# Sliding-window attention of block 1: two heads at a time in unrolled TensorE, VectorE and ScalarE steps, with the key projection moved first

## The reference, cut to what matters

```python
q, k, v = split(h @ w_qkv, [1024, 1280])
q = rms_norm(q per head, q_gain);  k = rms_norm(k per head, k_gain)
if latent: q, k = rope(q), rope(k)
q = q * 64 ** -0.5
s = concat(q @ kc.T, where(|t - s| <= 128, q @ kx.T, -inf))   # 512 keys
p = softmax(concat(sink, s))[1:]
o = p @ concat(vc, vx);   out = o @ w_out
```

## Time and profile before

| | us |
|---|---|
| median of 3 runs (4312.4 to 4322.81) | 4312.77 |
| the profiled execution: its own time | 4309.27 |
| the profiled execution: its span | 4307.5 |
| TensorE matmul busy | 3476.0 (81%) |
| VectorE busy | 1810.1 (42%) |
| ScalarE busy | 1109.1 (26%) |
| GpSimd busy | 1760.8 (41%) |

### The profile page before, as it was taken

How to read it: one execution, slowest core, us unless ns; L and a number is a source line. 1 busy time by engine, 2 the same in 40 slices (tenths; PEclk the granted TensorE clock), 3 DMA queues, 4 the chain that set the end, 5 groups by cost and what they waited for, 6 DMA issues and landing times.

```text
span 4307.5 us, 52062 instructions
## 1 busy us (share of the span) xinstructions
PE 3476.0 (81%) x20144; PEld 2893.3 (67%) x20144; DVE 1810.1 (42%) x2876; ACT 1109.1 (26%) x1485; POOL 1760.8 (41%) x1417
## 2 busy tenths in 40 slices
PE   6999897687875899989997566988666787776778
PEld 3777685576764577767886334988535777744677
DVE  2213386544446321232122534342256863234783
ACT  2222233111112221222222222333322332412332
POOL 1444341353442244434443003787014666403465
PEclk8999997798997999989998667998857898876889
DMA  6344221000000334333322001444202333310233
GB/s 241 137 161 140 81 97 50 1 1 1 1 1 1 107 135 163 129 121 134 115 91 102 10 0 39 161 161 143 86 9 78 117 123 131 120 59 33 104 112 112
DMA packets 58832, 388.59 MB, mean 90 GB/s; under 512 B 6432, under 2 KB 7712, under 8 KB 21184
## 3 DMA queue, kind: packets, MB, share of 16 engines
q1 hardware_dynamic: 49424, 320.49, 21.3%
q10 hardware_dynamic: 9072, 64.74, 4.2%
q0 software_dynamic: 192, 1.31, 0.1%
HBM read 385.47 MB, written 1.05 MB: 90 GB/s over the span
## 4 chain that ended last, share of the span: by engine, by line
PE 63%; DVE 13%; issue 11%; POOL 10%; ACT 1%; DMA 1%; POOLq 0%; DVEq 0%; SPq 0%; ACTq 0%
PE bank L550 15%; PE bank L551 14%; PE bank L552 14%; POOL ring_lo L1938 8%; DVE core L1844 2%; PE bank L752 2%; PE bank L750 2%; PE bank L742 1%; PE bank L575 1%; PE bank L859 1%; PE bank L845 1%; PE bank L923 1%; PE bank L568 1%; PE bank L838 1%; DVE h_hi L1441 1%
## 5 line engine op out<-in xcount | busy, mean ns | idle before, releaser
L1938 POOL TENSOR_TENSOR ring_lo<-ring,w_hi 128x512 fp32r<-128x512 f32 (+1 forms) x833 | 1086.5, 1334 | 1353.1 <-ACT w_hi L1052 1353.0
L552 PE MATMUL bank<-h_hi,ring_lo 128*128 128x256 f32 (+1 forms) x3376 | 1140.8, 338 | 0.0
L550 PE MATMUL bank<-h_hi,w_hi 128*128 128x512 f32 (+1 forms) x2448 | 885.6, 362 | 220.4 <-DVE h_lo L1443 96.2
L551 PE MATMUL bank<-h_lo,w_hi 128*128 128x512 f32 (+1 forms) x2448 | 864.6, 353 | 0.0
L552 PEld LDWEIGHTS bank<-h_hi,ring_lo 128*128 128x128 f32 x3376 | 678.8, 201 | 58.6
L550 PEld LDWEIGHTS bank<-h_hi,w_hi 128*128 128x128 f32 x2448 | 482.6, 197 | 322.0 <-issue 151.9
L551 PEld LDWEIGHTS bank<-h_lo,w_hi 128*128 128x128 f32 x2448 | 485.4, 198 | 51.1
L1052 ACT ACTIVATE w_hi<-ring 128x2048 fp32r<-128x2048 f32 (+2 forms) x227 | 394.8, 1742 | 465.2 <-PE bank L552 351.1
L552 PE MATMUL bank<-hid_r,ring_lo 128*128 128x256 f32 (+1 forms) x1088 | 365.6, 336 | 0.0
L1477 DVE SCALAR_TENSOR_TENSOR core<-core,bank 128x512 f32<-128x512 f32 (+1 forms) x88 | 54.6, 621 | 636.1 <-ACT core L1116 636.1
L550 PE MATMUL bank<-hid_r,w_hi 128*128 128x512 f32 (+1 forms) x808 | 290.5, 359 | 1.8 <-POOL ring_lo L1938 1.8
(11 more groups left out here) (347 smaller groups left out, 5916.3 us busy)
## 6 DMA issues: line engine op xcount, KB each, us to landing
ring<-w SPq DMA_DIRECT2D x88, 1024.0 KB, 4.8
zbuf<-ada_later ACTq DMA_DIRECT2D x60, 1024.0 KB, 4.8
ring<-up SPq DMA_DIRECT2D x48, 1024.0 KB, 4.8
ring<-w SPq DMA_DIRECT2D x64, 704.0 KB, 4.1
ring<-mla_in SPq DMA_DIRECT2D x30, 1024.0 KB, 4.8
ring<-down SPq DMA_DIRECT2D x32, 768.0 KB, 4.2
ring<-dn_in SPq DMA_DIRECT2D x16, 1024.0 KB, 4.8
ring<-ada SPq DMA_DIRECT2D x12, 1024.0 KB, 12.2
```

The source lines that it names most:

```text
L550: pe.matmul(out, a[0], b[0], start=start, stop=False)
L551: pe.matmul(out, a[0], b[1], start=False, stop=False)
L552: return pe.matmul(out, a[1], b[0], start=False, stop=stop)
L1938: ins = pool.tensor_tensor(like(ring_lo[:, r, a:b], part), like(ring[:, r, a:b], part), part.bitcast(F32), ALU.subtract)
```

## The change

- The columns of `swa_qk` are stored keys first, so slot 0 makes the two key chunks, and slots 1 to 4 the queries. GpSimd issues the load of the tables (`late`) ahead of its part in `swa_qk`, not behind it.
- ScalarE squares each chunk straight from PSUM as it copies it, and folds `q_gain` into the copy of a query chunk. TensorE's sums, and the rotations, stand between the slots of the projection. The sums of a query chunk are made with the squares as weights and two columns of the ones as the moving operand, which puts them on the partitions of the queries: 128 x 2 outputs for each 128 queries.
- Queries are rotated without their norm. The reciprocal root of each query and head goes into the scale of the exponential (`q_scale`), 16 columns at a time, and, negated, into its bias. Only the two key chunks still have a 512-wide reciprocal and scaling on VectorE.
- Attention is 16 pairs, written out without a loop. A pair is the two heads of one query chunk (partitions 0 to 63 and 64 to 127) and 128 queries. The mask is added on TensorE, by a matmul with the identity into the same PSUM region as the scores, for the one block of 128 keys that needs it. The maximum and the exponential read PSUM. The reciprocal of the sums is put on a diagonal (128 x 128), and a matmul of exponentials and diagonal turns and scales in one step.
- TensorE's turn t makes scores and mask of pair t, turns pair t-2, and multiplies pair t-3 with the values. Exponentials have three buffers. The chunks of `h` are split for the output projection inside the loop, and its first slot is prepared ahead of it. Staging copies on GpSimd are gone.

```diff
+                for n in range(5):
...
+                    if n == 1:
+                        pe.wait_ge(late_in, 32)
+                        key_sum(0)
+                    elif n == 2:
+                        key_sum(1)
+                        queries(0)
+                        queries(1)
+                    elif n >= 3:
+                        rotate(8 + n - 3)
+                        queries(2 * n - 4)
+                        queries(2 * n - 3)
...
+                def scores(p):
+                    c, j, kvp, _ = pair_of(p)
+                    pe.wait_ge(rope_done, max(ROTATED.index(c), ROTATED.index(8 + kvp)) + 1)
...
+                        pe.wait_ge(w_exped, p - 1)
...
+                        pe.matmul(bank(r)[:, :], sqk[rows, c, CTX + j * P:CTX + (j + 1) * P], sqk[rows, 8 + kvp, :],
+                                  start=True, stop=False)
+                    for r in range(2):
+                        mm = pe.matmul(bank(r)[:, m0:m0 + P], ident, late("s_mask", j * T + m0, P), start=False, stop=True)
+                def turned(p):
+                    for r in range(2):
+                        pe.wait_ge(w_scaled, 2 * p + r + 1)
+                        if p >= 1:
+                            pe.wait_ge(w_copied, 2 * p + r - 1)
+                        for c in range(4):
+                            mm = pe.matmul(psum[4 + r][:, c * P:(c + 1) * P], w_expo[:, p % 3, r, c * P:(c + 1) * P],
+                                           w_diag[:, p % 2, r, :], start=True, stop=True)
+                def values(p):
...
+                    for c in range(4):
+                        for r in range(2):
+                            kv = 2 * kvp + r
+                            mm = pe.matmul(psum[6 + p % 2][64 * r:64 * r + 64, 0:P], svt[:, c, kv * SD:(kv + 1) * SD],
+                                           w_probt[:, p % 2, r, c * P:(c + 1) * P], start=(c == 0), stop=(c == 3))
+                for t in range(PAIRS + 3):
+                    if t < PAIRS:
+                        scores(t)
+                    if 2 <= t < PAIRS + 2:
+                        turned(t - 2)
+                    if t >= 3:
+                        values(t - 3)
...
+                def take(n):
+                    act.wait_ge(slots_used, used("swa_qk", n))
...
+                        sq = act.activation(sqh[:, m % 4, t0:T], psum[m % 4][:, t0:T], ACT.Square)
...
+                def exps(p):
+                    act.wait_ge(w_maxed, p + 1)
...
+                        act.activation(w_expo[:, p % 3, r, :], psum[2 * (p % 2) + r][:, :], ACT.Exp,
+                                       scale=q_scale[:, 2 * p + r:2 * p + r + 1], bias=tok[:, W_NEG, 2 * p + r:2 * p + r + 1],
+                                       accum_out=tok[:, W_SUM, 2 * p + r:2 * p + r + 1])
+                    act.activation(w_small(W_SEXP, p), w_small(W_SARG, p), ACT.Exp).then_inc(w_exped, 1)
...
+                for t in range(PAIRS + 2):
+                    if t < PAIRS:
+                        exps(t)
+                    if t >= 2:
+                        copies(t - 2)
...
+                def maxes(p):
...
+                    for r in range(2):
+                        ins = dve.reduce_max(tok[:, W_MAX, 2 * p + r:2 * p + r + 1], psum[2 * (p % 2) + r][:, :], AX.X)
...
+                for t in range(PAIRS + 3):
+                    if t < PAIRS:
+                        maxes(t)
+                    if t == 2:
+                        query_scale(1)
+                    if 1 <= t < PAIRS + 1:
+                        scales(t - 1)
+                    if t >= 3:
+                        takes(t - 3)
...
-    a["swa_qk"] = tiles(np.concatenate([wq, w[:, 1024:1280]], 1), 256)
+    a["swa_qk"] = tiles(np.concatenate([w[:, 1024:1280], wq], 1), 256)
```

More of the change, by code:

```diff
@@ L822, in window @@
-                rotate(9)
-                pe.wait_ge(rope_done, 10)
-                for kvp in range(2):
-                    with pe.Fori(0, 2) as i:
-                        attend_pe(8, lambda U: U + i * 8 + kvp * 16, lambda u: scores(kvp, u),
-                                  lambda u: values(kvp, u), 4, lambda u: 2 * (kvp * 2 + i) + u // 4 + 1)
-                project_out("swa_out", X_BEFORE[4], hs, DC, 1, CTX, ready="swa_out")
-            def rotate(c):
-                pe.wait_ge(hnorm_done, 24 + c + 1)
-                if c >= 2:
-                    pe.wait_ge(rope_done, c - 1)
-                pe.matmul(psum[6 + c % 2][:, 0:SEQ], late("s_swap"), sqk[:, c, CTX:T], start=True, stop=True).then_inc(rot_done, 1)
@@ L836, in scores @@
-            def scores(kvp, u):
-                b, j, r = u // 4, u // 2 % 2, u % 2
-                pe.matmul(psum[u % 2][:, :], stage_q[64 * r:64 * r + 64, b, j * P:(j + 1) * P], sqk[64 * r:64 * r + 64, 8 + kvp, :],
-                          start=True, stop=True).then_inc(at["s"], 1)
-            def values(kvp, u):
-                r = u % 2
-                kv = 2 * kvp + r
-                for c in range(4):
-                    mm = pe.matmul(psum[4 + u % 2][64 * r:64 * r + 64, 0:P], svt[:, c, kv * SD:(kv + 1) * SD],
-                                   probt[:, u % 2, c * P:(c + 1) * P], start=(c == 0), stop=(c == 3))
-                mm.then_inc(at["o"], 1)
+                queries(6)
@@ L1505, in window @@
-                rope(9)
-                for kvp in range(2):
-                    with dve.Fori(0, 2) as i:
-                        sink_now[0] = (kvp, i)
-                        attend_dve(8, lambda U: U + i * 8 + kvp * 16, window_logits, window_norm,
-                                   lambda u: window_take(kvp, i, u))
-                for c in range(DC):
-                    dve.wait_ge(at["od"], CREDIT + 32)
-                    split("swa_out", c, h[:, c, CTX:T], CTX)
-                add_out("swa_out", k, 1, mod[:, k, 2, :], CTX)
@@ new lines, in window @@
+                rope(0, 0)
+                rope(1, 1)
+                key_norm(1)
+                for n, c in ((2, 8), (3, 2), (4, 3), (5, 9), (6, 4), (7, 5)):
+                    rope(n, c)
+                query_scale(0)
+                rope(8, 6)
+                rope(9, 7)
+                def maxes(p):
+                    c, j, kvp, c4 = pair_of(p)
+                    sink = POFF["sink"] + 8 * kvp + c4
+                    nsink = par[:, sink:sink + 5:4]
+                    dve.wait_ge(w_scored, p + 1)
+                    for r in range(2):
+                        ins = dve.reduce_max(tok[:, W_MAX, 2 * p + r:2 * p + r + 1], psum[2 * (p % 2) + r][:, :], AX.X)
+                    turn(ins)
+                    turn(dve.tensor_tensor(w_small(W_TMP, p), w_small(W_MAX, p), q_negscale[:, 2 * p:2 * p + 2], ALU.mult))
+                    turn(dve.tensor_tensor(w_small(W_NEG, p), w_small(W_TMP, p), nsink, ALU.min))
+                    dve.tensor_tensor(w_small(W_SARG, p), w_small(W_NEG, p), nsink, ALU.subtract).then_inc(w_maxed, 1)
@@ new lines, in scales, with takes @@
+                def scales(p):
+                    dve.wait_ge(w_exped, p + 1)
+                    turn(dve.tensor_tensor(w_small(W_TOT, p), w_small(W_SUM, p), w_small(W_SEXP, p), ALU.add))
+                    turn(dve.reciprocal(w_small(W_REC, p), w_small(W_TOT, p)))
+                    for r in range(2):
+                        dve.tensor_scalar(w_diag[:, p % 2, r, :], ident, tok[:, W_REC, 2 * p + r:2 * p + r + 1], None, ALU.mult)\
+                            .then_inc(w_scaled, 1)
+                def takes(p):
+                    c, j, _, _ = pair_of(p)
+                    dve.wait_ge(w_valued, p + 1)
+                    dve.tensor_copy(h[:, c, CTX + j * P:CTX + (j + 1) * P], psum[6 + p % 2][:, 0:P]).then_inc(w_taken, 1)
+                    if j == 1:
+                        dve.wait_ge(w_taken, p + 1)
+                        split("swa_out", c, h[:, c, CTX:T], CTX)
```

181 lines of the change are left out of this document (114 added, 67 removed).

## The result

| | before | changed |
|---|---|---|
| median, us | 4312.59 (4311.32 to 4322.81) | 4130.14 (4127.95 to 4134.46), 4 runs each |
| ratio, 95% interval | | 0.9573 (0.9557 to 0.959) |
| profiled execution: time, span, us | 4309.3, 4307.5 | 4127.95, 4126.1 |
| mean granted clock | 0.877 | 0.896 |

The kernel is 4.3% faster. The page of the changed kernel gives the chain that ended last, by engine; it answers to the earlier trace rows. TensorE's share rose from 63% to 65% and VectorE's fell from 13% to 11%.

The account below looks back on a forecast made before the run. TensorE's dense projections fill most of the program; in attention no engine is full, as engines hand one unit around. Attention -134, projections and rotations -32, behind attention -12: 4309.3 - 178 + 3.5 = 4135 us, range 4118 to 4196.

Parts of the forecast that it names:

- TensorE's sum for a pair: Attention loop: scores, masks, diagonals, values and idle time at 2.4 GHz sum to 4.7 us a pair.
- The idle time at each change of tile shape: Attention turn: TensorE idles 0.17 us between kinds of tile, three times a turn, 0.5 us in all.
- The loop through the engines: Attention: VectorE's maximum, ScalarE's exponentials and the copy freeing the bank take 4.7 us; 4.9 taken for two limits meeting.
- Attention: Whole attention stretch: 12.5 us for first turns, thirteen turns of 4.9, 6.5 to drain; 83 against 216.9, so -134.
- The transposes: Attention: diagonal matmuls replace transposes, speaking against the change; trace ratio 1.6 used, the skill's fourfold would put it near 4170.
- Projections and rotations: Stretch ahead of attention: first scores at about 2384 instead of 2416.5, -32 us; bounds 2378 and 2396.
- slot 0's double width: Projection: slot 0 becomes 512 wide at TensorE's low clock, costing between 0.6 and 5.7 us more; 3.6 taken.
- Behind attention: From last value to end of first output slot: 6 us instead of 17.8, -12, with splits made inside the loop.
- Rival 1: Attention: the clock stays low at 1.2 GHz, a turn costs 9.3 us, the kernel 4193; chance 0.12.
- Rival 2: Attention: value matmuls do not overlap, a turn is 5.6 us, the kernel 4145; chance 0.12.
- Rival 3: Projection waits for rotations: sixteen VectorE operations slowed beside GpSimd, up to 15 us, the kernel 4149; chance 0.13.
- Rival 4: Attention: pairs handed around without overlap, 18 us a turn, the kernel 4340 and slower than before; chance 0.03.

Follow-up runs that it names:

- e5: Changed kernel with the two mask matmuls of each pair left out: 4124.36 us, turns alternating between 4.35 and 4.07 us.
- e9: Changed kernel with exponentials scaled in place by VectorE, plain transposes instead of diagonal matmuls, and ScalarE's block copies ahead of its exponentials: 4113.64 us.
- e7: Changed kernel with only ScalarE's order altered, copying the turned blocks of pair t-2 before the exponentials of pair t: 4121.37 us.
- e4: Changed kernel with the splits of h and the first output slot's weight rounding moved back behind the last value: 4134.96 us.
- e1: Changed kernel with the eight value matmuls of a pair ordered head by head instead of alternating: 4136.6 us.
- e8: Changed kernel without the lag, every engine doing all steps of pair t in turn t: 4260.36 us, ratio 0.9879 to before.
- e10: The transposes kernel (e9) with the copy of the values out of PSUM moved from VectorE to ScalarE: 4114.84 us.
- e2: Changed kernel with each head's scores followed at once by its mask, so the two heads' scores do not stand together: 4151.33 us.

## Why the prediction was right

The forecast was 4135.0, and 4130.14 were measured. Its mechanism held and each of its stages came within 6 us. That the total came within 5 us is in part luck: the stages and what follows them gained more than forecast, and a step that nobody priced took 11 us back.

- **TensorE's sum for a pair**, 4.7: measured 4.51. Forecast and, in brackets, measured: scores 1.13 (1.06), masks 0.45 (0.54), diagonals 1.78 (1.88), values 0.9 (1.03), each right within 0.13. The idle time at each change of tile shape, 0.5 in the sum, isn't there: no row of a turn has any. (The five terms add up to 4.76, so 4.8 would have been the rounded sum.)
- **The loop through the engines**, 4.7: 4.35 (the stretched turns of e5). The prediction added 0.2 for two equal limits meeting. They aren't equal, and the turn is TensorE's sum alone. 4.9 was 0.4 too long.
- **Attention**, 83: measured 80.4. The first three turns took 13.1 us (forecast 12.5), the other thirteen 58.8 (63.7), and the last pairs' way out 8.5 (6.5): two errors that cancel in part. The clock of 0.85 or more came (0.96; 1.00 in the steady turns). TensorE is busy for 94%, where over 80% was forecast.
- **The transposes.** The prediction took the trace's ratio, 1.6 for a matmul against a transpose at the low clock, over the fourfold in the Trainium skill ("TensorE: Matmul & The Clock Gate", Terms). e9 measured both at the high clock: 1.88 / 0.97 = 1.9. The estimate of 4170 that the fourfold ratio gave was far off. That the diagonal speaks against the change, as the prediction said, is so: with transposes attention is 10.7 us shorter (e9 against e7).
- **Projections and rotations**, -32: measured -37.5. The first scores came at 2377.8, at the bound for "all of it hides" (2378) and not at 2384. The slots ended 3.2 to 4.8 us ahead of each stated time. The term that was mis-sized is slot 0's double width, 3.6: the slot took 23.0 us instead of 21.4, 1.6 more, because the clock rose inside it (0.70 in its stretch, 0.53 before). That is 2.0 of the 6.2 us by which the first scores came early. Of the rest, 1.2 is an earlier start, 1.6 are slots 1 to 3 (23.4 us against the 25 laid out; no run tells whether ScalarE's squares or something else was over-priced there), and 1.4 lie behind the values (3.6, laid out as 5).
- **Behind attention**, -12: measured -11.5. GpSimd ended slot 1's low part at 2458.83 + 5.22 = 2464.05, when slot 0 ended, as said. The prediction gave no price to GpSimd's low part of slot 0 in attention's first 5 us; it costs 1.3 us there (e4).
- **Rival 1** (low clock) was true of one turn of sixteen, 2.7 us. **Rival 2** (no overlap of values) was wrong, and its price too: e1 measured 5.00 a turn and not 5.6. **Rival 3** (16 slow rotation operations) happened in part, in rows of 1.40 to 1.52 for L1609, but nearly hidden: TensorE waited 1.1 us for this line between the slots and 1.8 ahead of the first scores. **Rival 4** was over-priced: e8 *is* a loop without overlap, and its turn is 13.65 and not 18, since TensorE is idle for 4.44 + 0.69 = 5.1 us of a turn and not for the 8.6 that the prediction made of VectorE's, ScalarE's and the hand-overs' time: the other head's work and the last copy lie beside TensorE's. That kernel is still faster than before (0.9879), so the rival's sign was wrong too.
- **What no step priced**: the 12 us operation. The prediction looked for stages that change and took the rest as fixed. It hid 11 us of the gain in the profiled execution; without it that execution would have taken near 4117 (4127.95 - 11.2), just below the low end of the range, 4118.

## To carry to other kernels

When a loop hands one unit around between engines, cost it twice: as the busiest engine's sum and as the way back to a buffer that is reused. Then run it lagged far enough for the sum to win: here taking the lag away cost 134 us of attention (214.0 against 80.1), 55 of them as TensorE's longer busy time (130.6 against 75.5 us), at a granted clock of 0.64 instead of 0.96. Compare stages of traces and not totals: moving the splits cost 9.7 us in the mixer and 4.8 in the total, and an edit that left the mixer's time alone (161.9 and 162.0) showed 7.9 in the total, with an operation of 12 us outside the mixer in one profile and not in the other.

## What the runs showed of the hardware

- One VectorE operation can last as long as about ten of GpSimd's subtractions in a row. Ordinarily a cast beside GpSimd's subtractions takes 1.35 us against 0.29 (e4). In five of the fourteen profiles one operation took 11.83 to 12.35 us. In all five it ended 0.15 to 0.29 us behind the end of a run of 20 subtractions that GpSimd made back to back (24.9 us). It was a CAST in four and a subtraction in one. All its operands are in SBUF. That GpSimd holds it up is read from this coincidence; no run took GpSimd's work away. In the other profiles GpSimd's rows are as dense (24 to 32 subtractions back to back), so what starts it isn't settled; the executions of e10 (4108.3 and 4109.17 against 4120.5 and 4120.98) suggest that it comes and goes within one kernel. The Trainium skill ("SBUF — State Buffer", "SBUF: two separate sides") describes an exclusive lock between the two engines for the length of one instruction; the wait over about ten is what the traces add.
- Column halves of 64 overlap only partly: eight values take 1.03 interleaved and 1.51 in a row (e1). Row halves overlap fully: two heads' scores take 1.13, one head's 1.12 (e2).
- A short wait of TensorE can cost a turn at the low clock, or not: after the same 3.4 us of waiting the clock fell to 0.54 for the third turn in the changed kernel, and stayed at 1.00 in e7. What decides was not tried.
- VectorE's smallest operations suffer beside GpSimd as well: an operation on 128x2 took 1.18 us instead of 0.16 in the changed kernel, and 0.16 in e4, where GpSimd was idle at that time.
